# Two MLPs of a split-precision transformer layer: the up products of w_hi taken as one 512-column product, the halves added afterwards

## The reference

```python
def swiglu(h, w_gu, w_down):              # first MLP, D_FF = 2816
    a, b = jnp.split(h @ w_gu, 2, axis=-1)
    return (jax.nn.silu(a) * b) @ w_down
# second MLP, D_FF_2 = 4096: relu(h @ w_up) squared, then @ w_down
```

## Time and profile before

| what | value |
|---|---|
| median of 3 runs | 816.05 us (815.46 to 817.51) |
| profiled execution, its own time | 815.42 us |
| span in its profile | 813.6 us |
| granted TensorE clock, mean | 0.999 of full |
| TensorE products (PE) | 786.7 us busy, 5493 instructions |
| weight loads (PEld) | 691.3 us busy |
| VectorE / ScalarE / GpSimd | 429.1 / 418.9 / 377.0 us busy |

### The profile page before, as it was taken

The page is one execution under the profiler, slowest core; times in us unless marked ns, Lnnn a source line. Parts: engine busy times, 40 slices in busy tenths (PEclk is TensorE's granted clock), DMA queues, the critical chain, the costliest instruction groups (busy, mean ns, idle before and its releaser), DMA issues.

```text
span 813.6 us, 14292 instructions
## 1 busy us (share of the span) xinstructions
PE 786.7 (97%) x5493; PEld 691.3 (85%) x5493; DVE 429.1 (53%) x684; ACT 418.9 (51%) x641; POOL 377.0 (46%) x181
## 2 busy tenths in 40 slices
PE   5999999999899999999999999999999999999996
PEld 3778877887677999999998889999897999999995
DVE  4676568984667633332336747645355343423435
ACT  5335426464846444544444955654766645444443
POOL 3126000000164754566545986565455554666452
PEclk9999999999999999999999999999999999999999
DMA  9984568133953666555654796434455556656551
GB/s 321 304 281 131 175 223 271 53 105 104 330 184 109 203 188 202 182 180 183 199 169 131 229 207 188 131 106 130 145 167 171 163 183 191 195 186 193 189 154 52
DMA packets 94396, 146.61 MB, mean 180 GB/s; under 512 B 15741, under 2 KB 64110, under 8 KB 94352
## 3 DMA queue, kind: packets, MB, share of 16 engines
q1 hardware_dynamic: 92896, 143.23, 56.3%
q0 software_dynamic: 1424, 2.77, 1.2%
q10 hardware_dynamic: 32, 0.01, 0.0%
HBM read 144.93 MB, written 1.06 MB: 179 GB/s over the span
## 4 chain that ended last, share of the span: by engine, by line
PE 80%; DVE 9%; issue 3%; ACT 2%; DMA 2%; POOL 2%; SPq 1%; DVEq 0%; ACTq 0%; POOLq 0%
PE bank L1881 78%; POOL w_lo L632 2%; ACT w_hi L697 1%; DMA raw<-in_w_mod 1%; DVE w_lo L1200 1%; PE bank L2151 1%; DVE hg_at L1436 1%; DVE hg_queries L1387 1%; DMA raw<-in_w_in 1%; SPq L554 1%; DMA gate_mlp_b<-gate_rows 1%; PE bank L2459 1%; DVE x L1833 1%; DVE stat L1517 1%; DVE hg_kf L1372 0%
## 5 line engine op out<-in xcount | busy, mean ns | idle before, releaser
L632 POOL TENSOR_TENSOR w_lo<-raw,w_hi 128x1024 fp32r<-128x1024 f32 (+2 forms) x150 | 361.8, 2429 | 311.4 <-ACT w_hi L697 309.4
L697 ACT ACTIVATE w_hi<-raw 128x1024 fp32r<-128x1024 f32 (+1 forms) x218 | 226.4, 1046 | 211.2 <-PE bank L1881 184.7
L1200 DVE TENSOR_TENSOR w_lo<-raw,w_hi 128x1024 fp32r<-128x1024 f32 x71 | 87.9, 1248 | 135.7 <-ACT w_hi L697 135.5
L1881 PE MATMUL bank<-z_hi,w_hi 128*128 128x256 f32 x384 | 109.0, 284 | 0.1
L1881 PE MATMUL bank<-z_lo,w_hi 128*128 128x256 f32 x384 | 107.5, 280 | 0.0
L1881 PE MATMUL bank<-z_hi,w_lo 128*128 128x256 f32 x384 | 107.5, 280 | 0.0
L1881 PE MATMUL bank<-n_hi,w_hi 128*128 128x256 f32 x352 | 99.1, 282 | 1.2 <-POOL w_lo L632 1.1
L1881 PE MATMUL bank<-n_lo,w_hi 128*128 128x256 f32 x352 | 98.6, 280 | 0.0
L1881 PE MATMUL bank<-n_hi,w_lo 128*128 128x256 f32 x352 | 98.6, 280 | 0.0
L1881 PE MATMUL bank<-w_hi,mlp_h_hi 128*128 128x512 f32 x216 | 84.2, 390 | 0.0
L1881 PE MATMUL bank<-w_lo,mlp_h_hi 128*128 128x512 f32 x216 | 84.1, 389 | 0.0
(11 more groups left out here) (419 smaller groups left out, 1590.9 us busy)
## 6 DMA issues: line engine op xcount, KB each, us to landing
raw<-in_w_in SPq DMA_DIRECT2D x54, 512.0 KB, 4.6
raw<-in_w_down SPq DMA_DIRECT2D x54, 512.0 KB, 3.6
raw<-in_w_gu SPq DMA_DIRECT2D x44, 512.0 KB, 3.5
raw<-in_w_up SPq DMA_DIRECT2D x32, 512.0 KB, 3.8
raw<-in_w_mod SPq DMA_DIRECT2D x24, 512.0 KB, 4.1
raw<-in_w_mod SPq DMA_DIRECT2D x32, 256.0 KB, 6.4
raw<-in_w_out SPq DMA_DIRECT2D x12, 512.0 KB, 4.0
raw<-in_w_in SPq DMA_DIRECT2D x8, 336.0 KB, 3.1
```

The costliest lines, as they stand in the source:

```text
L632: nc.gpsimd.tensor_tensor(wl[:, w % SPL, 0:size], raw[:, slot_raw, 0:size], wh[:, w % SPL, 0:size].bitcast(F32), ALU.subtract).then_inc(s_ ...
L697: nc.scalar.activation(wh[:, w % SPL, 0:size], raw[:, slot_raw, 0:size], ACT.Copy).then_inc(s_hi, 1)
L1200: V.tensor_tensor(wl[:, w % SPL, :], raw[:, slot_raw, :], wh[:, w % SPL, :].bitcast(F32), ALU.subtract).then_inc(s_lod, 1)
L1881: return nc.tensor.matmul(out_, l, r_, start=start, stop=stop, skip_group_check=True)
```

## The change

The three products of a pair (k, j) become two. `n_hi` and `n_lo` are now the two halves of one tile `n2` (in MLP 2 `y2`). `by_channel_wide` multiplies the stationary `w_hi` with both halves at once (512 moving columns), so that columns 0 to 255 of a bank collect hi*hi and columns 256 to 511 collect hi*lo; then `w_lo` with the high half is added into columns 256 to 511. A bank now holds one j only, so a group takes twice the banks: MLP 1 uses banks 0 and 1 for the gate and 2 and 3 for the up half in every group, MLP 2 uses banks 0 and 1 in every group.

The halves are added outside TensorE: ScalarE copies the two low halves to SBUF (`low_halves`, two copies of 128 x 256), VectorE adds the high halves from PSUM (`halves_added`, two additions). After that SiLU works in SBUF, MLP 1's multiplication has both operands in SBUF, and MLP 2's relu and square become one VectorE instruction with `max` and `mult`. TensorE starts the next up part after the additions (`s_usum`, `s_sum2`). The copy of `rowc` moves ahead, between ScalarE's copies of `n_hi`; some padding between tiles goes.

```diff
-            nc.scalar.activation(sg[:, 0, :], ps[0][:], ACT.Silu).then_inc(s_silu, 1)
+            low_halves(sg[:, 0, :], 0).then_inc(s_gcopy, 1)
+            low_halves(hm[:, 0, :], 2).then_inc(s_ucopy, 1)
+            silu(0, 0)
             h_hi(0, 0)
             with act.Fori(0, MLP1_TRIPS) as i:
                 for v in range(2):
                     g = 1 + v
-                    for c in range(2, 6):
+                    for c in range(2, 5):
                         hi_mlp(4 + 6 * v + c, i)
+                    act.wait_ge(s_used, W0 + 6 * g + 12 * i)
+                    low_halves(sg[:, 1 - v, :], 0).then_inc(s_gcopy, 1)
+                    hi_mlp(9 + 6 * v, i)
+                    silu(g, 1 - v, i)
                     act.wait_ge(s_used, W0 + 6 * g + 2 + 12 * i)
-                    act.wait_ge(s_h, g + 2 * i)
-                    nc.scalar.activation(sg[:, 1 - v, :], ps[2 * (1 - v)][:], ACT.Silu).then_inc(s_silu, 1)
+                    low_halves(hm[:, 1 - v, :], 2).then_inc(s_ucopy, 1)
                     hi_mlp(10 + 6 * v, i)
                     h_hi(g, 1 - v, i)
                     hi_mlp(11 + 6 * v, i)
...
+            def halves_added(dst, bank):
+                for j in range(2):
+                    ins = V.tensor_tensor(dst[:, T * j:T * j + T], ps[bank + j][:, 0:T], dst[:, T * j:T * j + T], ALU.add)
+                return ins
...
+            def mlp1(s, u, i=0):
+                dve.wait_ge(s_ucopy, s + 1 + 2 * i)
+                halves_added(hm[:, u, :], 2).then_inc(s_usum, 1)
+                dve.wait_ge(s_usum, s + 1 + 2 * i)
                 dve.wait_ge(s_silu, s + 1 + 2 * i)
-                V.tensor_tensor(hm[:, u, :], ps[2 * u + 1][:], sg[:, u, :], ALU.mult).then_inc(s_h, 1)
+                V.tensor_tensor(hm[:, u, :], hm[:, u, :], sg[:, u, :], ALU.mult).then_inc(s_h, 1)
...
             def mlp2(g, i=0):
-                dve.wait_ge(s_relu, g + 3 + 3 * i)
-                V.tensor_tensor(h2[:, g % 3, :], rr[:, g % 3, :], rr[:, g % 3, :], ALU.mult).then_inc(s_h2, 1)
+                dve.wait_ge(s_copy2, g + 1 + 3 * i)
+                halves_added(rr[:, g % 3, :], 0).then_inc(s_sum2, 1)
+                dve.wait_ge(s_sum2, g + 1 + 3 * i)
+                V.scalar_tensor_tensor(out=h2[:, g % 3, :], in0=rr[:, g % 3, :], scalar=0.0, in1=rr[:, g % 3, :],
+                                       op0=ALU.max, op1=ALU.mult).then_inc(s_h2, 1)
...
+            def by_channel_wide(s, k0, both, banks, made=None, order=(0, 1, 2, 3)):
+                for kk in order:
+                    k = k0 + kk
+                    if made:
+                        made(k)
+                    for j, bank in enumerate(banks):
+                        c = 256 * kk + P * j
+                        mm(ps[bank][:].rearrange("p (a t) -> p a t", a=2), wh[:, s, c:c + P], both[:, :, k, :], k == 0, False)
+                        ins = mm(ps[bank][:, T:2 * T], wl[:, s, c:c + P], both[:, 0, k, :], False, k == KT - 1)
+                return ins
```

More of the change, by code:

```diff
@@ L922, in _, with low_halves, silu @@
             hi_mlp(2)
-            for k in BY_BANK:
+            for c, k in enumerate(BY_BANK):
+                if c == 4:
+                    act.wait_ge(PE.sem, PE["mlp gate"])
+                    nc.scalar.activation(rowc[:, 0:T], ps[2][:, 0:T], ACT.Copy).then_inc(AC.sem, AC.tick("mlp gate"))
                 act.wait_ge(DV.sem, DV[f"n {k}"])
                 nc.scalar.activation(nh[:, k, :], ps[4 + k // 2][:, T * (k % 2):T * (k % 2) + T], ACT.Copy).then_inc(AC.sem, AC.tick(f"nh {k}"))
-            act.wait_ge(PE.sem, PE["mlp gate"])
-            nc.scalar.activation(rowc[:, 0:T], ps[2][:, 0:T], ACT.Copy).then_inc(AC.sem, AC.tick("mlp gate"))
+            def low_halves(dst, bank):
+                for j in range(2):
+                    ins = nc.scalar.activation(dst[:, T * j:T * j + T], ps[bank + j][:, T:2 * T], ACT.Copy)
+                return ins
+            def silu(g, u, i=0):
+                act.wait_ge(s_gsum, g + 1 + 2 * i)
+                nc.scalar.activation(sg[:, u, :], sg[:, u, :], ACT.Silu).then_inc(s_silu, 1)
             def h_hi(g, u, i=0):
@@ L1146, in relu @@
                     act.wait_ge(s_h2, g + 3 * i)
-                nc.scalar.activation(rr[:, g % 3, :], ps[g % 3][:], ACT.Relu).then_inc(s_relu, 3 if g == 0 else 1)
+                for j in range(2):
+                    ins = nc.scalar.activation(rr[:, g % 3, T * j:T * j + T], ps[j][:, T:2 * T], ACT.Copy)
+                ins.then_inc(s_copy2, 1)
             def h2_hi(g, i=0):
@@ L2304, in hidden_out, with up @@
                         ins.then_inc(PE.sem, PE.tick(f"{last} {t} {j}"))
-            def up(c, i, bank, first=False):
+            def up(c, i, first=False):
                 for n, q in enumerate((0, 2, 1, 3) if first else range(4)):
                     s = split(W0 + c + n, i, 12)
-                    by_channel(s, 4, 4 * (q % 2), nh, nl, T,
-                               [(ps[bank + q // 2][:, T * j:T * j + T], j == 0) for j in range(2)],
-                               (lambda k: pe.wait_ge(DV.sem, DV[f"nl {k}"])) if first and q < 2 else None, BY_BANK[0:4]).then_inc(s_used, 1)
+                    if first and q == 2:
+                        pe.wait_ge(AC.sem, AC["mlp gate"])
+                    by_channel_wide(s, 4 * (q % 2), n2, (2 * (q // 2), 2 * (q // 2) + 1),
+                                    (lambda k: pe.wait_ge(DV.sem, DV[f"nl {k}"])) if first and q < 2 else None,
+                                    BY_BANK[0:4]).then_inc(s_used, 1)
             def down(c, i, g, u, first=False, last=False):
@@ L2317, in down @@
                 hidden_out(mh[:, u, :], ml[:, u, :], lambda q: split(W0 + c + q, i, 12), last and "mlp")
-            up(0, 0, 0, first=True)
+            up(0, 0, first=True)
             pe.wait_ge(s_h, 1)
@@ L2516, in _, with up2 @@
                 keep_clock(1, 1 if t else 4)
-            def up2(c, g, i=0, first=False):
+            def up2(c, i=0, first=False):
                 for q in range(2):
                     s = split(M0W + c + q, i, 12)
-                    by_channel(s, 4, 4 * q, zh, zl, T, [(ps[g % 3][:, T * j:T * j + T], j == 0) for j in range(2)],
-                               (lambda k: pe.wait_ge(DV.sem, DV[f"yl {k}"])) if first else None, BY_BANK[0:4]).then_inc(s_used, 1)
+                    by_channel_wide(s, 4 * q, y2, (0, 1), (lambda k: pe.wait_ge(DV.sem, DV[f"yl {k}"])) if first else None,
+                                    BY_BANK[0:4]).then_inc(s_used, 1)
             def down2(c, g, i=0, last=False):
```

82 lines of the change are left out of this document (45 added, 37 removed).

## The result

The changed kernel takes 819.15 us (median of 8 runs, 818.7 to 820.81); the kernel before took 817.29 us in the same session (8 runs, 815.46 to 817.78). The ratio is 1.0033, with a 95% interval from 1.0024 to 1.0042: slower, by 1.9 us between these medians and by 2.7 us by the ratio. The forecast was 814.9 us, and "no change that can be told" was its likeliest case. The time lies inside the range of 811 to 820 us and at the value of rival 4.

A forecast was written before the change was run, and what follows sets the result against it. It took TensorE's product pitches to bound both loops, with waits at the MLPs' edges paid in full. 815.42 - 4.4 + 0 + 3.15 = 814.2 us, plus 0.63 to the median, gave 814.9 us; range 811 to 820.

The forecast's parts named there:

- rival 4: TensorE's up parts: cost follows columns, the pair stays near 0.3534 us, only edge costs remain; 819 us, chance 0.08.
- Term 1: TensorE's up parts in both MLPs: a pair falls from 0.3534 (MLP 1) to 0.3449 us, saving 4.4 us.
- upper bound: TensorE's up parts: highest cost taken for a pair, 0.2317 + 0.1200 = 0.3517 us, leaving -0.5 us.
- Term 2: Steady groups: the added ScalarE and VectorE copies and additions never stall TensorE; 0 us.
- rival 2: Steady groups: GpSimd wins the lock and VectorE's multiplication waits; +17.5 us, 832 us, chance 0.08.
- Term 3: Starts and ends of both MLPs: delays there are paid in full; +3.15 us, between 1.5 and 4.5.
- (a): MLP 1's start: earlier low part, but TensorE waits for copies and additions to about 263.6 us; -0.1 us.
- (b): MLP 1's first loop group: GpSimd's subtraction holds the multiplication, so a low part comes late; +1.3 us.
- (d): MLP 2's start: group 0's squaring, the sums of squares and `w_hi` come later; +0.9 us.
- (e): MLP 2's end: the last subtraction waits for GpSimd, delaying VectorE's last low part; +0.55 us.
- (c): MLP 1's end: the multiplication holds the low part ahead of the gate rows' DMA; +0.5 us.
- Rival 3: Up parts: two-piece operand slows the wide product, or pair 0.3517 and edges 4.5 us; 820 us, chance 0.14.

The follow-up runs named there:

- padded: The changed kernel with the 48-word paddings back ahead of `n_hi_lo` and `y_hi_lo`: 819.37 us.
- three_narrow: The changed kernel with the wide product cut back into two narrow ones, everything else of the change kept: 822.67 us.
- twos: The changed kernel with both paddings back and the two wide products of a k-tile issued ahead of its two narrow ones: 816.02 us.
- padded_wides_first: The changed kernel with the padding back and, in each chunk, 8 wide products issued before its 8 narrow ones: 815.95 us.
- one_piece: The changed kernel with high and low of a k-tile stored side by side, so the 512 moving columns are one piece: 819.08 us.
- before_unpadded: The kernel before with the 48 words ahead of `n_hi` taken out and those ahead of `z_hi` moved behind `z_lo`: 820.93 us.
- E: Stream of 32 wide `w_hi` products alone, added to the changed kernel ahead of MLP 1's last down part: 0.2278 us each.
- F: Stream of 32 narrow `w_lo` products alone, added to the changed kernel ahead of MLP 1's last down part: 0.1200 us each.
- G: Stream of 32 steps of three narrow products, as in the kernel before, added to the changed kernel at MLP 1's end: 0.3600 us a step.
- wide_only: The changed kernel without the `w_lo` products of the up parts, so only wide products follow one another: 776.28 us (one run).
- edges_after: The changed kernel with ScalarE's `mlp_h_hi` copy behind the next `w_hi`, and MLP 2's starting sums of squares ahead of group 0's copies: 818.74 us.

## Why the prediction was wrong

- **Term 1 failed.** It priced the pair at 0.2271 + 0.1178 = 0.3449 us and expected -4.4 us; the pair costs 0.353 us and the products give some 0.3 us in all (0.01 to 0.02 in each steady up part). The step that failed is the sum of two pitches taken from streams of one kind, although "no row shows the two kinds in turn". Taken strictly in turn they cost 0.0055 us a pair more than the sum of their streams (0.3534 against 0.3478). The rest of the miss is the pitches themselves: on these operands they are 0.2278 and 0.1200, and not 0.2271 and 0.1178. Its upper bound, 0.3517, was too low as well: it summed slower rows but left no room for a cost of the order.
- **The padding was not priced.** The section on the change names it, and the working passes over it. Its removal costs 0.20 us in an up part of the kernel before, 0.0021 us a narrow product, and 4.9 us in all (820.93 us against 816.07). In the changed kernel it happens to cost nothing, since the strict turn of wide and narrow holds the pair at 0.353 with or without it (padded). With the padding the two streams add up to 0.3512 and the strict turn adds 0.002, without it to 0.3478 and the turn adds 0.0055. It made three_narrow hard to read.
- **In the best order** the pair comes to 0.347 us (twos, padded_wides_first). Term 1 is then -0.2 us per group of MLP 1, and 3.4 us between the medians of padded and padded_wides_first; it pays for the edges and no more: 815.95 us. That is near the outcome forecast, by a kernel that was not the one proposed, and by luck in the parts: wide products at 0.2334 in place of 0.2271 us, narrow ones at 0.1135 in place of 0.1178 where they follow one another.
- **Term 2 was right.** No steady up part has a gap. The multiplication starts 1.68 us behind the first down product (forecast 1.75) ahead of GpSimd at 1.88, and runs in 0.69 us; rival 2 did not occur. Unforeseen are 0.06 us per down part in MLP 1 and 0.03 in MLP 2, some 1 us together. With the padding they are 0.03 in both, with the wide products first as well 0.01 to 0.02; what makes them is not shown.
- **Term 3 was right in place and nearly in size.** (a) and (b) together: 26.21 against 24.78 us from the first up product to the first down product, 1.43 where 1.2 was forecast. The multiplication was held by the subtraction just as (b) says, but that the sum fits is in part luck. The first loop product starts 13.99 us behind the first up product and not 13.77, 0.2 us later, where (a) had 0.1 earlier; the wait for the low part is 0.9 us where (b) had 1.3; and 0.3 us is no wait at all but pitch: this up part ran at 0.1136 us a product before and runs at 0.353 a pair now, a loss of term 1. (d) 13.14 against 12.29: 0.85 (0.9). (e) 18.16 against 17.75: 0.41 (0.55). (c): the DMA of the gate rows starts 432.55 - 427.96 = 4.59 us behind the first down product, against 429.74 - 425.48 = 4.26 before, so 0.33 (0.5), and one_piece's stretch is longer by 0.3. The stretch of the profiled run is longer by 1.49, mostly since that DMA took 5.87 us in it; it took 4.64 to 4.90 us in the profiles of the kernel before, one_piece, padded, before_unpadded, twos and padded_wides_first.
- **The sum** of what was measured is -0.3 (steady up parts) + 1.0 (down parts) + 1.43 + 0.85 + 0.41 + 0.3 (c) = 3.7 us, and one_piece's span is longer by 3.6; the forecast had -4.4 + 3.15.
- **Rival 4 came about** in its time and in its first half: the pair stays at 0.353. Its reason is not shown. "Cost follows columns" does not fit E + F = 0.3478 against G = 0.3600, the same 768 columns in the same kernel. And the rule of the Trainium skill in "TensorE: Matmul & The Clock Gate" (Back-to-back issue gap), one fixed 2.5 ns per product, which that section gives for a product taken by itself, names neither the order of the products nor the address of the operand. By it the pair would cost 0.325 us, an estimate by that page; no loop or stream of wide and narrow products here costs less than 0.346 a pair. The measurement decides.
- **Rival 3** ended nearest in the wide pitch: with the padding it is 0.2334 us and not 0.2271. Without it the same two pieces run at 0.227 (wide_only) and 0.2278 (stream E), so the two pieces alone do not cost this; an operand in one piece was not run with the padding. The rival's threshold, a loss from a pair of 0.3545 us on, does not follow from its own rows: -0.5 us at 0.3517 and 560 steady and first loop pairs put it near 0.3526, where the measured 0.353 already lies.

## What to carry to other kernels

A gain of a few per cent in a product's pitch can't be read off streams of one kind: measure the very sequence, with the operands where the kernel will have them, in a stream that the kernel has room for. When a change removes padding or moves a tile, put that part back by itself before believing any other explanation. A price at an edge (an instruction that comes to share a lock, a queue that waits behind it) is worked out well from the timeline; mending it needs the same care, since the stall can move on to the next instruction, as it did in edges_after.

## What the runs showed of the hardware

- A wide and a narrow product strictly in turn: 0.3531 to 0.3534 us, whichever bank, columns or weights (but 0.347 in the first stream of all); two and two: 0.3484, the sum of the separate streams to 0.0006. This is without the padding; with it the strict turn is 0.3532, the sum 0.3512, and two and two in the kernel 0.347.
- A shift of the moving operand by 48 words: narrow 0.1200 to 0.1178 us, wide 0.2278 to 0.2334 us. The two move in opposite directions. The granted clock was 1.00 in all these stretches.
- The same three-narrow stream ran at 0.1178 us a product behind an alternating stream and at 0.1134 behind a wide one, in one execution, with no other compute engine at work. Why is open.
- VectorE's multiplication with two SBUF operands, 0.69 us by itself, was recorded with 2.35 us when one GpSimd subtraction was under way and none was ready behind it, and with 4.71 us when another was ready: VectorE did not get in between them. That a VectorE instruction with two SBUF inputs and a GpSimd one that reads SBUF contend for an exclusive lock, held by whichever starts first, is what the Trainium skill's page "SBUF — State Buffer" (Who interferes with whom) states. The trace agrees, and adds that a waiting VectorE can be passed over. It is not always: in the steady groups `mlp_h_lo`, started at 296.69 us, waited for the first of two GpSimd subtractions and ended at 298.81, though the second was ready; that one ended at 301.06.
